# Spreading the setup work of one DeltaNet inverse over neighbouring schedule steps: key products one head a step, clamps one direction a step, one mask product a step later

## The reference

```
decay = exp(gc_i - gc_j)              (j before i)
A     = I + strict(beta_i * (k_i . k_j) * decay)      and its inverse, applied to beta*v and beta*exp(gc)*k
qk    = (q_i . k_j) * decay
```

## The kernel before

| k | PE | ACT | POOL | DVE |
|---|---|---|---|---|
| 0 | | `tt_cols` = beta matrix, 4 heads (L1269) | | |
| 1 | | clamp: `relu(gc - decay)` of 4 heads into `x_w`, then of 4 heads into `t_cols` (L1277) | | |
| 2 | `products`: 4 heads, keys times keys and queries (L2860) | | `x_w += t_cols` (L2286) | |
| 3 | | `x_w = exp(-x_w)` (L1282) | | |
| 4 | | | `tt_cols *= x_w` (L2289) | |
| 5 | | | | `m_t` = kk * `tt_cols` (L2094), `p_all` = qk * `x_w` (L2096) |
| 6 | | packs the 32x32 diagonal blocks of `m_t` into row 1 of `x_w` (L1286) | | |
| 7 | | | | first inverse from the packed blocks (L2100, L2103), transpose (L2114), two sides (L2116) |
| 8 to 15 | 32 products of 32x32 a stage, even stages L2869, odd L2876 | | | even: L2107; odd: L2111, transpose L2114, sides L2116 |
| 16, 17 | L2884 and L2896; L2902, then L2909 | L1290 | | 17: L2120 |
| 18, 19 | L2920; L2928 (64x64 blocks) | L1293, L1297; L1303 | | |

## Time and profile before

### The profile page before, as it was taken

How to read it: one execution, slowest core, us unless ns; L and a number is a source line. 1 busy time by engine, 2 the same in 40 slices (tenths; PEclk the granted TensorE clock), 3 DMA queues, 4 the chain that set the end, 5 groups by cost and what they waited for, 6 DMA issues and landing times.

```text
span 1544.5 us, 31492 instructions
## 1 busy us (share of the span) xinstructions
PE 1458.2 (94%) x12718; PEld 1350.8 (87%) x12718; DVE 1009.0 (65%) x1893; ACT 620.6 (40%) x1240; POOL 107.1 (7%) x88
## 2 busy tenths in 40 slices
PE   7899999999999999999996777899999999999998
PEld 2899999999999999887785556799999999998886
DVE  4977777777465747552886675478877777753333
ACT  4522222221122533442556555554544444444223
POOL 0000000000000000020002113553000000000000
PEclk9999999999999999998998776999999999999999
DMA  9344454445244222212101110111122223222222
GB/s 346 104 143 150 139 159 149 149 137 163 95 137 143 76 68 69 55 55 56 42 1 63 45 39 11 36 56 55 55 69 82 81 86 91 82 68 69 82 69 96
DMA packets 174589, 141.70 MB, mean 92 GB/s; under 512 B 8464, under 2 KB 156437, under 8 KB 173461
## 3 DMA queue, kind: packets, MB, share of 16 engines
q1 hardware_dynamic: 151652, 117.63, 24.5%
q10 hardware_dynamic: 22833, 22.59, 4.7%
HBM read 136.75 MB, written 3.45 MB: 91 GB/s over the span
## 4 chain that ended last, share of the span: by engine, by line
PE 83%; DVE 10%; issue 2%; ACT 2%; SPq 1%; DMA 1%; DVEq 0%; ACTq 0%
PE ps L2317 15%; PE ps L2318 14%; PE ps L2319 14%; PE ps L2469 5%; PE ps L2467 5%; PE ps L2468 5%; PE ps L2539 3%; PE ps L2537 3%; PE ps L2538 3%; PE ps L2959 1%; PE ps L2747 1%; PE ps L2768 1%; PE ps L2973 1%; PE ps L2944 1%; DVE tt_cols L2116 1%
## 5 line engine op out<-in xcount | busy, mean ns | idle before, releaser
L2317 PE MATMUL ps<-h_hi,w_lo 128*128 128x320 f32 x1152 | 366.5, 318 | 12.2 <-DVE h_lo L1445 4.5
L2318 PE MATMUL ps<-h_lo,w_hi 128*128 128x320 f32 x1152 | 358.5, 311 | 0.0
L2319 PE MATMUL ps<-h_hi,w_hi 128*128 128x320 f32 x1152 | 358.3, 311 | 0.0
L1398 DVE TENSOR_TENSOR w_lo<-w_raw,w_hi 128x1024 fp32r<-128x1024 f32 x120 | 148.1, 1236 | 233.3 <-ACT w_hi L742 233.0
L2317 PEld LDWEIGHTS ps<-h_hi,w_lo 128*128 128x128 f32 x1152 | 218.5, 190 | 19.6 <-issue 8.1
L2318 PEld LDWEIGHTS ps<-h_lo,w_hi 128*128 128x128 f32 x1152 | 218.9, 190 | 0.8 <-issue 0.2
L2319 PEld LDWEIGHTS ps<-h_hi,w_hi 128*128 128x128 f32 x1152 | 218.5, 190 | 0.0
L742 ACT CAST w_hi<-w_raw 128x1024 fp32r<-128x1024 f32 x120 | 125.5, 1047 | 198.8 <-PE ps L2319 109.3
L1532 DVE SCALAR_TENSOR_TENSOR ada_acc<-ada_ffn,cond,ada_acc 128x256 f32<-128x256 f32 x392 | 161.8, 479 | 1.2
L2317 PE MATMUL ps<-act_hi,w_lo 128*128 128x320 f32 (+1 forms) x352 | 108.9, 309 | 2.1 <-DVE mods L1561 2.1
L2318 PE MATMUL ps<-act_lo,w_hi 128*128 128x320 f32 (+1 forms) x352 | 108.5, 308 | 0.0
(11 more groups left out here) (425 smaller groups left out, 2909.2 us busy)
## 6 DMA issues: line engine op xcount, KB each, us to landing
w_raw<-in_w_ffn_in SPq DMA_DIRECT2D x64, 512.0 KB, 3.9
w_raw<-in_w_ffn_out SPq DMA_DIRECT2D x44, 512.0 KB, 3.7
ada_ffn<-in_w_ada ACTq DMA_DIRECT2D x43, 512.0 KB, 4.0
w_raw<-in_w_in SPq DMA_DIRECT2D x28, 512.0 KB, 3.7
ada_ffn<-in_w_ffn_in SPq DMA_DIRECT2D x20, 512.0 KB, 3.8
ada_k<-in_w_ada SPq DMA_DIRECT2D x8, 1024.0 KB, 10.6
ada_ffn<-in_w_ada SPq DMA_DIRECT2D x13, 512.0 KB, 3.4
w_raw<-in_w_out SPq DMA_DIRECT2D x8, 512.0 KB, 3.4
```

Source lines behind the costliest of these rows:

```text
L1398: nc.vector.tensor_tensor(w_lo[at], w_raw[s][:], w_hi[at].bitcast(F32), ALU.subtract)\
L2317: nc.tensor.matmul(out, lo, xh, start=start, stop=False)
L2318: nc.tensor.matmul(out, hi, xl, start=False, stop=False)
L2319: return nc.tensor.matmul(out, hi, xh, start=False, stop=stop)
```

## The change

Five moves, nothing is added to or taken from the arithmetic:

- `products` takes one head; it is called in the stages k = 1, 2, 3 and 4. The wait for the unit before of the same set (or for the copied keys and values) moves from k = 2 to k = 1, the mark `t_pe` stays with head 3, now at k = 4.
- ACT's clamps: `x_w` at k = 1, `t_cols` at k = 2.
- ACT's exponential moves from k = 3 to k = 4.
- DVE's product for `p_all` (queries times keys, times decay) moves from k = 5 to k = 6.
- ACT's packed blocks go to row 2 of `t_cols` instead of row 1 of `x_w`, and ACT waits for `m_t` alone (DVE mark 1 instead of 2). The readers (DVE at k = 7, `inner_first` on PE) follow.

```diff
@@ ACT
                 if k == 1:
                     act.wait_ge(chain_in[c], 32 * r + 32)
-                    for d, x in ((0, x_w[c]), (1, t_cols[c])):
-                        q = 8 * d + 4 * g
-                        for h in range(4):
-                            ins = nc.scalar.activation(x[:, h, :], x[:, h, :], ACT.Relu,
-                                                       bias=gc[:, t, q + h:q + h + 1], scale=-1.0)
-                        ins.then_inc(t_act[c], 1)
-                if k == 3:
+                if k in (1, 2):
+                    d, x = ((0, x_w[c]), (1, t_cols[c]))[k - 1]
+                    q = 8 * d + 4 * g
+                    for h in range(4):
+                        ins = nc.scalar.activation(x[:, h, :], x[:, h, :], ACT.Relu,
+                                                   bias=gc[:, t, q + h:q + h + 1], scale=-1.0)
+                    ins.then_inc(t_act[c], 1)
+                if k == 4:
                     act.wait_ge(t_pool[c], r * POOL_T + 1)
                     nc.scalar.activation(x_w[c][:], x_w[c][:], ACT.Exp, scale=-1.0).then_inc(t_act[c], 1)
                 if k == 6:
-                    act.wait_ge(t_dve[c], r * DVE_T + 2)
+                    act.wait_ge(t_dve[c], r * DVE_T + 1)
                     for a in range(0, P, SUB):
-                        ins = nc.scalar.copy(heads4(x_w[c][a:a + SUB, 1, :], SUB), m_t[c][a:a + SUB, :, a:a + SUB])
+                        ins = nc.scalar.copy(heads4(t_cols[c][a:a + SUB, 2, :], SUB), m_t[c][a:a + SUB, :, a:a + SUB])
                     ins.then_inc(t_act[c], 1)
@@ DVE
                 if k == 5:
                     dve.wait_ge(t_pe[c], pe0 + 1)
                     dve.wait_ge(t_pool[c], r * POOL_T + 2)
-                    (m_t product, then p_all product)
+                    (m_t product)
+                if k == 6:
+                    (p_all product)
                 if k == 7:
                     dve.wait_ge(t_act[c], act0 + 5)
-                    nc.vector.tensor_tensor(heads4(t_now, SUB), heads4(x_w[c][:, 1, :], SUB), packed("level0", 4),
+                    nc.vector.tensor_tensor(heads4(t_now, SUB), heads4(t_cols[c][:, 2, :], SUB), packed("level0", 4),
                                             ALU.mult).then_inc(t_dve[c], 1)
@@ PE
-            def products(t, g, c):
-
-                for h in range(4):
-                    rows = slice((h % 2) * DK, (h % 2) * DK + DK)
-                    at = 2 * g + h // 2
-                    both = pre[rows, at:at + 5:4, t * P:(t + 1) * P]
-                    out = heads4(ps[:, 2 * c + h % 2, :], P)[:, h // 2:h // 2 + 3:2, :]
-                    ins = nc.tensor.matmul(out, qk(t, g, h, 4), both, start=True, stop=True)
-                ins.then_inc(t_pe[c], 1)
+            def products(t, g, c, h):
+
+                rows = slice((h % 2) * DK, (h % 2) * DK + DK)
+                at = 2 * g + h // 2
+                both = pre[rows, at:at + 5:4, t * P:(t + 1) * P]
+                out = heads4(ps[:, 2 * c + h % 2, :], P)[:, h // 2:h // 2 + 3:2, :]
+                ins = nc.tensor.matmul(out, qk(t, g, h, 4), both, start=True, stop=True)
+                if h == 3:
+                    ins.then_inc(t_pe[c], 1)
@@ PE, inner_first
-                        ins = nc.tensor.matmul(blocks_of(ps[:, 2 * c, 0:P], a, h), blocks_of(x_w[c][:, 1, :], a, h),
+                        ins = nc.tensor.matmul(blocks_of(ps[:, 2 * c, 0:P], a, h), blocks_of(t_cols[c][:, 2, :], a, h),
                                                blocks_of(tt_cols[c][:, 0, :], a, h), start=True, stop=True)
@@ PE, schedule
-                if k == 2:
+                if k == 1:
                     if r >= 1:
                         pe.wait_ge(t_act[c], act0)
                     elif c >= 1:
                         pe.wait_ge(kv_copied, 4 if c == 1 else 2 * NT + 2)
-                    products(t, g, c)
+                if 1 <= k <= 4:
+                    products(t, g, c, k - 1)
```

More of the change, by code:

```diff
@@ L2064, in scan_out, with by_pair, by_pair_of @@
                 nc.vector.tensor_tensor(out, out if s in (0, 3, 4) else oq[b], ps[:, 4 + b, 256:512], ALU.add).then_inc(c_dve[b], 1)
+            def by_pair(x):
+                return x.rearrange("p (h e) n -> p e h n", e=2)
+            def by_pair_of(x):
+                return x.rearrange("p e (h n) -> p e h n", n=P)
             for k, c, r, t, g in make_schedule():
@@ L2091, in _ @@
                     dve.wait_ge(t_pool[c], r * POOL_T + 2)
[L2092 to L2097, removed]
+                    nc.vector.tensor_tensor(by_pair(m_t[c][:]), by_pair_of(ps[:, bank:bank + 2, 256:512]), by_pair(tt_cols[c][:]),
+                                            ALU.mult).then_inc(t_dve[c], 1)
+                if k == 6:
+                    nc.vector.tensor_tensor(by_pair(heads4(p_all[:, t, g, :], P)), by_pair_of(ps[:, bank:bank + 2, 0:256]),
+                                            by_pair(x_w[c][:]), ALU.mult).then_inc(t_dve[c], 1)
                 if k == 7:
                     dve.wait_ge(t_act[c], act0 + 5)
-                    nc.vector.tensor_tensor(heads4(t_now, SUB), heads4(x_w[c][:, 1, :], SUB), packed("level0", 4),
+                    nc.vector.tensor_tensor(heads4(t_now, SUB), heads4(t_cols[c][:, 2, :], SUB), packed("level0", 4),
                                             ALU.mult).then_inc(t_dve[c], 1)
```

## The result

The changed kernel takes 1561.8 us in the median of 7 runs (1553.78 to 1566.81) against 1547.66 us (7 runs): ratio 1.0089, 95% interval 1.0064 to 1.0115, that is 14 us slower, 10 to 18. The forecast was 1553.0 us, range 1539 to 1560. The direction was right; the forecast rise of 6.7 us was half of the 14 us measured.

The account below looks back on a forecast made before the run. The prediction took the ten units' stage to be bound by a loop of waits between PE and DVE. It summed 10.7 - 3.1 - 0.9 = +6.7 us onto 1546.29 us, giving 1553.0 us, range 1539 to 1560.

Parts of the forecast that it names:

- The stage is a loop between PE and DVE, and it alone moves: Ten units' stage: PE products and DVE masks wait in turn; scan and output projection behind shift one for one.
- Different heads share the array; a head alone costs 1.15 us: Key products on PE: a lone head has no partner, 1.15 us at the lower clock, 0.65 us at the upper.
- The first rival: Key products: the two instructions of one head run side by side, 0.73 us alone; 1544.9 us, chance 0.19.
- The clock: Units' stage on PE: places priced at the existing mix of 2.4 and 1.2 GHz, granted clock expected unchanged.
- The granted clock of 840 to 960 us as before: Sign in the units' stage: granted clock unchanged there; near 0.8 would mean the clock had gone up.
- The rival on the clock: Units' stage: steadier PE work holds the clock at its upper level, -6.4 us, 1539.9 us; chance 0.18.
- the 6.7 us of the sum: Whole kernel: 10.7 us for the key products less 3.1 for `p_all` and 0.9 for the clamps, slower.
- 17 places uncovered, 11 with partial cover, 18.6 us in all: 40 lone-head places on PE: 17 cost 15.0 us, 11 cost 3.6, 12 nothing; 18.6 replaces 7.9 us, +10.7.
- `p_all` gains 3.1 us: DVE between `m_t` and the older units' mask: moving `p_all` behind that mask gains 3.1 us, bounds 0 and 4.2.
- Clamps gain 0.9 us, exponential and wait cost nothing: ACT in step 2: moved clamps gain 0.9 us, bounds 0 and 1.26; later exponential and moved PE wait cost 0.
- POOL being late: Rival, units 2 to 8: POOL's product lands on older units' sides and `m_t` waits; 1558.4 us, chance 0.08.
- The drain: PE tiling changes: full 0.65 us on both sides of 30 added entries, some 10 us, left out of the sum.

Follow-up runs that it names:

- e3: Changed kernel with two places instead of four: heads 0 and 1 (different 64 partitions) at stage 2, heads 2 and 3 at stage 3; ratio 0.9967 to the kernel before.
- e4: Changed kernel with two places, each holding heads of the same 64 partitions: 0 and 2 at stage 2, 1 and 3 at stage 3; ratio 1.0042.
- e5: Changed kernel with four places, each running a pair (0 and 1 twice, 2 and 3 twice), so every key product is computed twice; ratio 0.9993.
- e8: Changed kernel with four places, the second and fourth with their partner computed again, the first and third alone; ratio 0.9991.
- e1: Kernel before with the split alone: one head's key product in each of stages 1 to 4, no other moves; ratio 1.0076.
- e9: Kernel before with only `p_all` a stage later and the packed blocks in the other row; key products together, old clamps and exponential; ratio 0.9962.
- e10: Changed kernel with true pairs at stages 2 and 3, and clamps and exponential back in their old places; ratio 0.9964.
- e14: Changed kernel with each head's product issued twice in its place, on the same 64 rows; ratio 1.0155.
- e11: Kernel before with true pairs of heads at stages 2 and 3 and nothing else moved; ratio 0.9989.

## Why the prediction was wrong

Point by point, by its own steps:

- *The stage is a loop between PE and DVE, and it alone moves.* Right: 13.4 us of the spans' difference arise before the scan (17.4 in the stage, less 4.0 of an earlier start).
- *Different heads share the array; a head alone costs 1.15 us.* Right to the hundredth: 1.22 us with 0.07 overlapped. Shown by e3 against e4, and by e5's places of the same length as lone ones. The first rival (the pair is inside one head) is out.
- *The clock.* This is the step that failed. The prediction priced the places at the mix of levels that the kernel before had, and wrote of its check "The granted clock of 840 to 960 us as before". It fell to 0.50 in most windows, and from 840 to 960 us to 0.53 from 0.68. The rival on the clock looked only upwards, with a chance of 0.18, and no case had it falling. The partner that a lone head lacks was counted as time alone; e5 and e8 show that giving it back brings the clock back, and 15 us with it.
- *What the fall costs.* A lone head costs 1.15 instead of 0.65 us, a group of 32 block products 0.65 instead of 0.45. The runs split the 14 us in three: the changed kernel against e5, the same four places without partners, +15 us; e5 against e3, four places instead of two, +4 us; e3 against the kernel before, -5 us. The second figure is net of e5's higher clock; in the profiles e5's stage (816.2 to 990.0, 173.8 us) is 7.3 us longer than e3's (816.0 to 982.5, 166.5 us).
- *The same by the clock alone.* A second estimate comes from the kernel before itself: over 33 runs of the same instructions its time follows its mean clock over the whole span, from 1542.41 us at 0.966 to 1555.03 at 0.953, 0.80 us for each 0.001 (correlation -0.88; on three other chips 0.84 to 0.92 us, one execution with 0.914 set aside). From 0.960 to 0.946 that makes 14 x 0.80 = 11 us of the 14, and 3 us would be left at an equal clock. That is a correlation, carried beyond the lowest clock it was taken from: the changed kernel's one execution with 0.958 took 1553.78 us, the kernel before's six with 0.958 took 1545.66 to 1550.44 us, so some 5 us, not far from the 6.7 us of the sum. For e1, without the other moves, the same line leaves nothing. So the sum may have been near at an unchanged clock, but that its terms were right one by one is not shown.
- *17 places uncovered, 11 with partial cover, 18.6 us in all.* The count was good (27 on the chain, 28 forecast). The sum was not: 29.8 us on the chain, nearly all at full price; the likely reason, not tested by itself, is that at the lower clock the idle time that should have covered them was gone. In unit 4 the first was to cost 0.47 and the third 0.2 us; they stand with 0.63 and 1.15. The chain's length of the places is not their marginal cost, so I read it as a sign only.
- *`p_all` gains 3.1 us.* The mechanism is seen in one place, 0.59 us of the 0.6 forecast; e9 gave 5.9 us, 4 of which may be clock. Beside the split neither this nor the 0.9 us of the clamps showed, since the changed kernel is not faster than e1. The runs do not say why.
- *Clamps gain 0.9 us, exponential and wait cost nothing.* Not contradicted (e10 against e3), too small to be measured. POOL being late did not show up: from 815 to 1000 us the changed kernel's DVE has no idle time that POOL ended.
- *The drain.* The Trainium skill ("TensorEngine Tiling (Array Packing)", Key Properties) says that a change of the tiling mode drains TensorE. That its full price on both sides of 30 more entries would be 10 us was left out of the sum. e5 has these entries and is 4 us behind e3, which has 10 of them, so 10 us for it are not seen here, and a smaller price stays possible.

Not settled is what it is in a stretch of lone heads that leaves the clock down. Busy time in the windows above does not tell the cases apart; e14 shows that doubling the work on the same rows does not bring back what partners do; e8 that two partners of four do as well as four.

## What to carry to other kernels

Before a group of small matmuls is split for a smoother schedule, look whether its members share the array: two on different 64 rows took the time of one. Split along pairs, not through them. And where TensorE runs near the change between its two levels, price a change of its list at both, downwards too: here a forecast of 7 us became 14.

Moving a DVE operation that nobody waits for from ahead of a waited-for mask to behind it gave 6 us (e9, with the packed blocks that it needs); the best rearrangement on PE alone gave 2 us (e11), which can't be told from nothing.

## What the runs showed of the hardware

- A 64-row float32 matmul of 256 columns (two instructions) runs beside one on the other 64 rows at no cost: 1.22 us alone and 1.23 us with partner at the lower clock, 0.70 us both at the upper. Two on the same rows take 2.07 us at the lower clock.
- Partners need not be neighbours in the kernel's list: the order 0, 2, 1, 3 takes 2.08 us like 0, 1, 2, 3.
- More work made the kernel faster: 80 added instructions that ride along (e5 has 160 instead of 80) went with a granted clock of the stage of 0.75 instead of 0.56 (median over the span 0.971 instead of 0.946) and took 15 us off.
- More busy time of PE did not go with a higher granted clock: 0.52 at 137 us busy of 160 (e4), 0.73 at 112 (before), 0.75 at 123 (e5).
- The time of one unchanged kernel follows its mean granted clock: 0.80 us for each 0.001 over 33 executions, which is most of its spread of 13 us.
